# Seams between the stages of a four-layer network: the last weight slots by halves, turned rows of one half made meanwhile, mixers begun from rows without the root, layers unrolled

## The reference

```python
x = x + 0.5 * swiglu(rms_norm(x, g1), w_gate, w_up, w_down)      # FFN, 1024 -> 2816 -> 1024
x = x + mixer(rms_norm(x, g2))                                   # w_in, four branches or attention, w_out
x = x + 0.5 * swiglu(rms_norm(x, g3), ...)                       # a second FFN
```

## Time and profile before

| | |
|---|---|
| runs | 2213.47, 2214.14, 2214.24 us |
| median | 2214.14 us |
| profiled execution | 2215.12 us |
| its span, first to last instruction | 2213.3 us |
| TensorE matmuls busy | 2135.7 us, 96% |
| GpSimd busy | 1650.7 us, 75% |
| VectorE, ScalarE busy | 1015.2 us (46%), 996.0 us (45%) |
| HBM | 165 GB/s over the span |
| granted TensorE clock | 0.988 of full, mean |

### The profile page before, as it was taken

The page is one execution under the profiler, slowest core; times in us unless marked ns, Lnnn a source line. Parts: engine busy times, 40 slices in busy tenths (PEclk is TensorE's granted clock), DMA queues, the critical chain, the costliest instruction groups (busy, mean ns, idle before and its releaser), DMA issues.

```text
span 2213.3 us, 43461 instructions
## 1 busy us (share of the span) xinstructions
PE 2135.7 (96%) x15448; PEld 1965.4 (89%) x15448; DVE 1015.2 (46%) x1544; ACT 996.0 (45%) x1637; POOL 1650.7 (75%) x682
## 2 busy tenths in 40 slices
PE   7998999999999899999999989999999998999997
PEld 7998998999899898899899978889989997888997
DVE  3445545434443554434444454544444444454444
ACT  5344444434443544434444455444444445544343
POOL 6886855888788675688788854668878886466887
PEclk9999999999999999999999999999999999999999
DMA  6554533555455453455555543345555554334554
GB/s 223 189 180 154 183 116 123 189 182 188 155 187 182 153 172 115 143 182 188 180 171 186 169 163 111 130 153 187 182 179 164 188 174 162 108 132 153 189 181 142
DMA packets 101335, 365.72 MB, mean 165 GB/s; under 512 B 11888, under 2 KB 12528, under 8 KB 100976
## 3 DMA queue, kind: packets, MB, share of 16 engines
q1 hardware_dynamic: 101088, 363.20, 49.9%
q10 hardware_dynamic: 144, 1.19, 0.1%
HBM read 363.29 MB, written 1.05 MB: 165 GB/s over the span
## 4 chain that ended last, share of the span: by engine, by line
PE 92%; DVE 3%; issue 2%; ACT 2%; DMA 0%; SPq 0%; ACTq 0%; DVEq 0%
PE twin L559 19%; PE twin L561 18%; PE twin L560 18%; PE twin L593 9%; PE twin L594 9%; PE twin L595 8%; PE twin L680 1%; PE twin L574 1%; PE twin L663 1%; PE twin L575 1%; PE twin L576 1%; DVE stat L1459 1%; PE twin L606 1%; DVE stat L1461 1%; PE twin L669 1%
## 5 line engine op out<-in xcount | busy, mean ns | idle before, releaser
L524 POOL TENSOR_TENSOR wlo<-raw,whi 128x1024 fp32r<-128x1024 f32 x678 | 1650.5, 2459 | 554.3 <-ACT whi L1143 553.5
L559 PE MATMUL twin<-thi,whi 128*128 128x256 f32 x3504 | 1000.4, 286 | 14.7 <-DVE tlo L1475 14.7
L561 PE MATMUL twin<-thi,wlo 128*128 128x256 f32 x3504 | 992.0, 283 | 0.0
L560 PE MATMUL twin<-tlo,whi 128*128 128x256 f32 x3504 | 991.5, 283 | 0.0
L1143 ACT CAST whi<-raw 128x1024 fp32r<-128x1024 f32 x686 | 696.4, 1044 | 45.9 <-PE twin L595 28.7
L559 PEld LDWEIGHTS twin<-thi,whi 128*128 128x128 f32 x3504 | 672.6, 192 | 27.8 <-issue 19.5
L560 PEld LDWEIGHTS twin<-tlo,whi 128*128 128x128 f32 x3504 | 672.4, 192 | 8.8 <-issue 1.0
L561 PEld LDWEIGHTS twin<-thi,wlo 128*128 128x128 f32 x3504 | 672.2, 192 | 0.0
L1515 DVE TENSOR_TENSOR hlo<-mix,hhi 128x256 fp32r<-128x256 f32 x176 | 393.4, 2235 | 133.9 <-ACT hhi L1192 133.9
L1188 ACT ACTIVATE mix<-mix 128x256 f32<-128x256 f32 x176 | 73.6, 418 | 815.7 <-DVE mix L1510 815.7
L1510 DVE TENSOR_TENSOR mix<-twin,root 128x512 f32<-128x512 f32 x176 | 121.7, 692 | 618.9 <-PE twin L561 607.3
(11 more groups left out here) (265 smaller groups left out, 1468.3 us busy)
## 6 DMA issues: line engine op xcount, KB each, us to landing
raw<-in_w_dram SPq DMA_DIRECT2D x686, 512.0 KB, 3.3
con<-in_con_dram ACTq DMA_DIRECT2D x1, 1161.5 KB, 7.9
x<-in_x_dram SPq DMA_DIRECT2D x1, 1024.0 KB, 4.8
out_dram<-xs SPq DMA_DIRECT2D x4, 256.0 KB, 2.7
mix<-in_last_gain_dram SPq DMA_DIRECT2D x1, 512.0 KB, 3.5
par<-in_par_dram SPq DMA_DIRECT2D x2, 208.0 KB, 3.1
par<-in_par_dram SPq DMA_DIRECT2D x2, 154.0 KB, 3.0
gain<-in_gain_dram SPq DMA_DIRECT2D x5, 12.0 KB, 2.8
```

Of the source, the lines that this page charges most:

```text
L524: nc.gpsimd.tensor_tensor(wlo[:, place, :], raw[:, place, :], whi[:, place, :].bitcast(F32), ALU.subtract).then_inc(split_done, 1)
L559: pe.matmul(out, hi, thi[:, k, :], start=(k == 0), stop=False)
L560: pe.matmul(out, hi, tlo[:, k, :], start=False, stop=False)
L561: mm = pe.matmul(out, lo, thi[:, k, :], start=False, stop=(k == KD - 1))
```

## The change: what it does, and the diff

- **Tail.** The last three down slots of an FFN (19, 20, 21) are put behind gate/up 21, and run half 0 of all three, then half 1 of all three; the same for the last two slots of w_out. After the first of them has done its half 1, TensorE turns half 0 of the new x (8 transposes). Step 21 keeps its rows in a third place of `hhi`/`hlo`. In the very last FFN the slots run by token tile instead (`last_tail`).
- **Head.** The first two slots of each stage run in four parts: slot 0's lower four k, the 8 transposes of half 1, slot 1's lower four k, slot 0's and slot 1's upper four k. Turned rows of w = 1 and 2 go to `yhi`/`ylo` and new tiles `ehi`/`elo`.
- **Root.** The chain works in a PSUM bank but for its result, and has four small instructions more; squares come behind the upper parts of their half. The root is spread from `stat` itself, without a diagonal, in the middle of slot 2.
- **Mixers.** They begin like an FFN, from rows with gain but without the root, for slots 0 to 3; their results are multiplied by the root afterwards in PSUM (`rooted`). Meanwhile the turned x, still in its banks, is multiplied by gain and root and split again (`normalised`), and slots 4 on use that. Convolutions, rotations and pairs of the start come 2 to 4 slots later; in the second mixer the compressed k and v tile comes before the gates.
- **Ring and layers.** The ring's left-out places are spread over the mixer; GpSimd splits all slots; the four empty slots are gone. The loops over layers are written out; the loops inside the FFNs stay, one turn shorter.
- **End.** Per token tile: add, square, root, wait for the last gain, two results.

```diff
-TAIL = AHEAD
-IP_BANK1 = [5 + m % 2 for m in range(CHUNKS1 // 2)]
+IP_BANK1 = [6, 5, 4, 7] + [5 + m % 2 for m in range(4, CHUNKS1 // 2)]
-SHARED = [[FFN_SLOTS, FFN_SLOTS + 2], [FFN_SLOTS, FFN_SLOTS + 2]]
+SKIPS = {MIX1: (8, 14, 20, 26), MIX2: (8, 14, 22)}
...
+            def head(L, w, n, out):
+                ready = lambda j: early_ready(pe, L, w, j)
+                first, second = out[:, 0:SEQ], out[:, SEQ:2 * SEQ]
+                low, high = range(KD // 2), range(KD // 2, KD)
+                wait_slot(L, n)
+                fm_part(L, n, first, low, w, True, False, ready)
+                x_turned(L, w, 1)
+                wait_slot(L, n + 1)
+                fm_part(L, n + 1, second, low, w, False, False)
+                fm_part(L, n, first, high, w, False, True, ready).then_inc(slot_used, 1)
+                fm_part(L, n + 1, second, high, w, False, True).then_inc(slot_used, 1)
+            def root_spread(L, w, name):
+                out = claim(pe, L, name)
+                pe.wait_ge(ev("root_ready"), 3 * L.deep + w + 1)
+                for T in range(NT):
+                    mm = pe.matmul(out[:, T * P:(T + 1) * P], stat[:, T:T + 1].to_broadcast([P, P]), ident, start=(T == 0), stop=True,
+                                   skip_group_check=True)
+                full(L, name, mm)
...
+            def tail(L, slots, acc, next_norm):
+                last = slots[-1][0]
+                for half in range(2):
+                    for n, ahi, alo, inputs_ready in slots:
+                        if half == 0:
+                            inputs_ready()
+                            wait_slot(L, n)
                         for T in range(NT):
+                            mm = acc_part(L, n, ahi, alo, acc, half, T, False, n == last)
+                        if half == 1:
+                            mm.then_inc(slot_used, 1)
+                            if n == slots[0][0]:
+                                x_turned(*next_norm, 0)
...
+                head(L, 2 * f, base, bank[b])
+                gate_up(2, 1, 0, midway=lambda: root_spread(L, 2 * f, ("R", f)))
                 down(4, 0, first=True)
-                with pe.Fori(0, STEPS // 2 - 1) as i:
+                with pe.Fori(0, STEPS // 2 - 2) as i:
                     gate_up(5, 0, i + 1, i)
                     down(7, 1, i)
                     gate_up(8, 1, i + 1, i)
                     down(10, 2, i)
-                down(FFN_SLOTS - 1, STEPS - 1, last=True)
+                gate_up(FFN_SLOTS - 7, 0, STEPS // 2 - 1)
+                gate_up(FFN_SLOTS - 5, 1, STEPS // 2 - 1)
...
+            def norm(L, w, soon):
+                upper_x(L, w, 0)
+                for n in soon:
+                    split_hi(L, n)
+                squares(L, w, 0)
+                upper_x(L, w, 1)
+                squares(L, w, 1)
+                split_hi(L, ffn_slot(L, w))
+            def normalised(L):
+                root_kept(L, ("R", "mix"))
+                for j in range(KD // 2):
+                    act.wait_ge(ev("rescaled"), 4 * L.deep + j + 1)
+                    nc.scalar.copy(thi[:, 2 * j:2 * j + 2, :], psum(L, ("norm", 1, j))[:].rearrange("p (k n) -> p k n", k=2)).then_inc(ev("upper_again"), 1)
+                    if j < 3:
+                        split_hi(L, FFN_SLOTS + AHEAD + 1 + j)
...
-                step(0, STEPS - 2, STEPS // 2 - 1, (n - 2,), (n - 1, n) if f else (n - 1,))
-                step(1, STEPS - 1, STEPS // 2 - 1, (), (n + 1, n + 2, n + 3) if f else ())
+                step(0, STEPS - 2, STEPS // 2 - 1, (n - 2,), (n - 1,) if last else (n - 1, n))
+                step(1, STEPS - 1, STEPS // 2 - 1, (), () if last else (n + 1, n + 2), at=2 * SEQ)
...
+            def roots(own, squares_done, ready, scratch, tiles=range(NT)):
+                dve.wait_ge(sq_done, squares_done)
+                n, first = len(tiles), tiles[0]
+                zero, v, t, vh = (scratch[:, 2 * i:2 * i + n] for i in range(4))
+                y = stat[:, first:first + n]
...
+            def norm(L, own, w, added=None):
+                for half in range(2):
+                    if added is not None:
+                        add_to_x(*added, half)
+                    lower_x(L, w, half)
+                roots(own, L.deep * (6 * NT) + (w + 1) * 2 * NT, ev("root_ready"), bank[7])
+            def normalised(L):
+                wait_drained(dve, L, ("R", "mix"))
+                def scaled(j):
+                    out = psum(L, ("norm", 1, j))
+                    for c in range(2):
+                        part = out[:, c * SEQ:(c + 1) * SEQ]
+                        ins = dve.scalar_tensor_tensor(part, part, gain_of(L, 1, 2 * j + c), root[:], ALU.mult, ALU.mult)
+                    ins.then_inc(ev("rescaled"), 1)
+                def lower(j):
+                    dve.wait_ge(ev("upper_again"), 4 * L.deep + j + 1)
+                    drained(L, ("norm", 1, j), dve.tensor_tensor(tlo[:, 2 * j:2 * j + 2, :], psum(L, ("norm", 1, j))[:].rearrange("p (k n) -> p k n", k=2),
+                                                                 thi[:, 2 * j:2 * j + 2, :].bitcast(F32), ALU.subtract))
+                scaled(0)
+                for j in range(1, KD // 2):
+                    scaled(j)
+                    lower(j - 1)
+                lower(KD // 2 - 1)
+            def rooted(own, L, m):
+                out = psum(L, ("ip", m))[:].rearrange("p (t n) -> p t n", t=2)
+                own.link(dve.tensor_tensor(out, out, root[:].unsqueeze(1).to_broadcast([P, 2, SEQ]), ALU.mult))
...
             for T in range(NT):
                 for half in range(2):
+                    add_to_x(end, lambda T, half: ("acc", 1, T, half), 0.5, half, (T,))
+                roots(own, 2 * DEPTH * 6 * NT + 2 * (T + 1), ev("last_root"), bank[4], (T,))
+                dve.wait_ge(ev("last_root"), T + 1)
+                dve.wait_ge(s_par, 16 * 2 * DEPTH + 16)
+                for half in range(2):
                     cols = slice(half * 512, half * 512 + 512)
```

More of the change, by code:

```diff
@@ L444, in build @@
         y_moba = xs[:].rearrange("p t n -> p (t n)")[:, 1024:2048]
+        layers = [Layer(l, blk) for blk in range(2) for l in range(DEPTH)]
+        behind = dict(zip(range(len(layers)), layers[1:]))
         block = ctx.enter_context(nc.Block())
@@ L496, in _ @@
             sp.dma_start(gain[:], gain_d[0]).then_inc(s_gain, 16)
-            with sp.Fori(0, DEPTH) as l:
-                layer(l, 0)
-            with sp.Fori(0, DEPTH) as l:
-                layer(l, 1)
+            for blk in range(2):
+                for l in range(DEPTH):
+                    layer(l, blk)
             last = Layer(DEPTH, 1)
-            for n in range(TAIL):
-                load(last, n)
             sp.wait_ge(slot_used, last.slot0 + RING)
@@ new lines, in fm_part @@
+            def fm_part(L, n, out, ks, w, start, stop, ready=None):
+                r = L.pos[n] % RING
+                for k in ks:
+                    xhi, xlo = turned_x(w, k)
+                    if ready is not None and k % 2 == 0:
+                        ready(k // 2)
+                    hi, lo = whi[:, r, k * P:(k + 1) * P], wlo[:, r, k * P:(k + 1) * P]
+                    pe.matmul(out, hi, xhi, start=start and k == 0, stop=False, skip_group_check=True)
+                    pe.matmul(out, hi, xlo, start=False, stop=False, skip_group_check=True)
+                    mm = pe.matmul(out, lo, xhi, start=False, stop=stop and k == KD - 1, skip_group_check=True)
+                return mm
@@ new lines, in last_tail @@
+            def last_tail(L, slots, acc):
+                last = slots[-1][0]
+                for T in range(NT):
+                    for n, ahi, alo, inputs_ready in slots:
+                        if T == 0:
+                            inputs_ready()
+                            wait_slot(L, n)
+                        for half in range(2):
+                            mm = acc_part(L, n, ahi, alo, acc, half, T, False, n == last)
+                        if T == NT - 1:
+                            mm.then_inc(slot_used, 1)
@@ L1456, in roots, with lower_x @@
                 for step in range(3):
-                    for T in range(NT):
-                        c = slice(T, T + 1)
-                        own.step(dve.scalar_tensor_tensor(t[:, c], y[:, c], vh[:, c], y[:, c], ALU.mult, ALU.mult))
-                    own.wait()
-                    ins = dve.scalar_tensor_tensor(y, t, 1.5, y, ALU.add, ALU.mult)
-                    if step == 2 and ready is not None:
-                        ins.then_inc(ready, 1)
-                        dve.wait_ge(ready, own.L.each)
-                    else:
-                        own.link(ins)
-                return y
-            def remainders(L, w):
-                for j in range(KD // 2):
+                    own.link(dve.tensor_tensor(t, vh, y, ALU.mult))
+                    own.link(dve.tensor_tensor(t, t, y, ALU.mult))
+                    if step < 2:
```

(4 more changed lines are left out.)

449 lines of the change are left out of this document (216 added, 233 removed).

## The result

The kernel after takes **2176.01 us** (median of four runs, 2175.85 to 2176.86) against 2213.9 for the kernel before beside it (four runs, 2213.47 to 2214.24): ratio 0.983, 95% interval 0.9813 to 0.9847. The forecast was 2183.5, the range 2168 to 2199. The profiled execution spans 2174.0 us, so the span lost 39.3 us where the sum had 30.6.

What follows compares the result with a forecast made beforehand. TensorE busy 96% of the span, savings only at seams, start and end. Gains 21.4 (mixer heads) + 12.3 (FFN heads) - 3.1 (start and end) = 30.6 us off median 2214.14: 2183.5 us, range 2168 to 2199.

Steps and rivals of the forecast that it cites:

- (a): FFN tails by halves: TensorE waits 1.6 us for the last hlo at seven tails, 11 us; bounds 0.7 and 12.
- Rival A: Tail does not meet GpSimd, so the 11 us come too: 2173 us; chance 0.18.
- (b): Stage heads: upper four k about 0.3 us late behind an FFN; all waits 1.2 us behind a mixer.
- (c): Root at seams: PSUM chain takes 3.0 us, no wait; bound 24 us if a 2.3 us stall came back.
- (d): Rescaled rows in mixers: waits 1.8 us, gate logits' source 0.8 us late in first mixers; bound 0 to 3 us more.
- (e): GpSimd takes back the 8 slots VectorE split, 2.46 us each: costs nothing.
- (f): Layers unrolled: the layer loop's two turns cost 3.4 us together, counted inside the FFN seams' 22.8 us.
- (g): Start: 8 transposes now stand between matmuls at the low clock, 1.8 us; loss 0.5 us.
- (h): End: VectorE waits for the last gain before taking up tile 1; loss 2.6 us, bounds 0 and 4.
- Rival B: Start of the mixers costs 3 us more each: 2195 us, or 2200 with a late root; chance 0.21.
- Rival C: Mixers' 12 VectorE rescaling instructions stuck behind GpSimd's splits, 2.0 us more each, 96 us: 2279 us; chance 0.05.
- Rival D: Seams do not shorten, each wait goes to the next producer: within 4 us of 2214; chance 0.04.

Runs made afterwards that it cites:

- e1: Kernel after with the next stage's first weight split moved behind step 21, leaving two splits, not three, behind step 20: 2164.67 us, ratio 0.9778.
- e6: Kernel after with the 8 transposes of half 1 ahead of the first slot's matmuls, not between them: 2191.6 us, ratio 0.9894.
- e3: Kernel after with the root's chain in SBUF scratch again, not in a PSUM bank: 2199.19 us, ratio 0.9935.
- e4: Kernel before with only its loops over layers written out: 2206.26 us, ratio 0.9966.
- e10: Kernel after, unchanged, run once more in a second set: 2175.71 us, ratio 0.9831.
- e2: Kernel after with the last gain asked for 12 slots before the end, not behind the last slot: 2172.97 us, ratio 0.9816.
- e5: Kernel after with the last slots run whole, slot by slot, and half 0 turned only behind the last: 2185.06 us, ratio 0.987.
- e8: Kernel after with the edits of e1 and e2, and tile 1's adds between tile 0's root and its results: 2160.17 us, ratio 0.9758.
- e7: Kernel after with the head's rescaling taken out, so mixers wait for the root and all slots use rescaled rows: 2221.66 us, ratio 1.0036.

## Why the prediction was right, and where it was not

The sign, the mechanism and the range held, and the row that the forecast was built around came as told. The sum was short by 8.7 us (39.3 for 30.6), and that it was not short by more is luck: some 16 us came that it had not counted on, and some 7 went that it had not counted either. By its steps:

**(a) Tail by halves: right, to 0.1 us.** The step had to choose between a wait of 0.1 and one of 1.6 us, and took 1.6; the excess is 1.63 to 1.70 seven times, hlo took 2.06 us, and e1 shows that GpSimd was the cause. The choice between the two ends was made by where the batch stood in the earlier trace rows, and that is what decided. Rival A did not happen; that 2176.0 lies nearer to its 2173 than to 2183.5 is because of other terms.

**(b) Head: mis-sized, in the safe direction.** The 0.3 us behind an FFN is 0.15, at the first of the upper four k (213.40 and not 213.25, 0.05 us after `elo` is released), and the 1.2 us behind a mixer is 0.85 (0.27 at the first slot, 0.43 at the transposes, 0.15 at the upper four k): 7 x 0.15 + 4 x 0.35 = 2.4 us more gain. e6 shows that the head by quarters is needed for it.

**(c) Root: right.** The root is there 0.5 us before TensorE wants it, where the sum had 0.3. The "nothing" that this step cost was worth 23 us: e3 takes it back.

**(d) Rescaled rows: right in mechanism, too dear.** The four pairs were put 3.3, 4.8, 6.4 and 8.2 us behind the spread; they are ready after 3.4, 4.9, 6.3 and 7.7. The term that was too dear is the cycle of a pair, 0.44 + 0.44 + 0.69 = 1.57 us: the instructions overlap by 0.06 to 0.08 us each, and the `tlo` rows start 1.40 to 1.44 us apart. TensorE also comes to the first pair 4.7 us behind the spread (222.53) and not 4.3. Waits are 0.82 us in a first mixer (0.20 at 224.17, 0.62 at 225.60) and 0.97 in a second, and not 1.8, so 3.6 us in four mixers; the wait for the gate logits' source, 0.8 us in the two first mixers, isn't in the list: 1.6. The step also said that "the second mixer's rotations make their dates". There something was missed. L709 is the matmul that opens a bank of scores with the mask, L719 turns the exponentials that ScalarE makes of the scores (L1431). In the two second mixers they stand idle for 5.3 us in 10 pieces. The lines of before that answer to them are L653 and L663; the first had 1.5 us in 2 pieces (further down the list of the earlier trace rows), the second none. With 0.16 us a piece that is 6.9 against 1.8: 5.1 us against. This was a step passed without a number, and no run here takes it apart.

**(e) GpSimd's eight slots: right.** No row of the mixers waits for GpSimd; the only wait for wlo is at the start.

**(f) Unrolling: the sum held, its price was seen wrong.** It was put inside the 22.8 us and told as 3.4 us. e4 alone gives 7.2. The seams' sum was unhurt, because it was taken from all waits there and not from the "issue" row; the start's part was missed. The Trainium skill (Runtime: NRT & Kernel Launch, Instruction fetch mechanics) says that a taken branch to code outside the small window must fetch it before execution goes on; this fits the direction of e4, but no run here shows that the fetch is the cause. The amount at one turn, 3.1 us, is from the rows above.

**(g) Start: wrong in sign.** A loss of 0.5 us was forecast. The first gate matmul comes at 15.74 and not at 17.62, and 12 weight matmuls go at half clock and not 27, against which stand the transposes between (18.44 to 19.59). The 144th gate or up matmul starts at 38.90 and not 40.70: 1.8 us gained, so 2.3 us more than forecast. In e4 it starts at 39.18, in e10 at 39.19: 1.5 us goes with the unrolled code, and not with the order of squares that this step argued about. The shorter spell is not in e4, which again has 27 slow matmuls, and its cause was not found.

**(h) End: right, 1.0 us too dear.** From the last matmul's start to the end it was 12.9 us and is 14.4; forecast loss 2.6, measured 1.5 to 1.6. e2 shows that the late gain was its cause: 3.0 us come back.

**Two terms outside the steps.** One is a gain. In the kernel after, matmuls of 256 columns that read the new tiles `yhi`, `ylo`, `ehi` and `elo` (the first slots of a mixer, and every gate and up slot of the FFN behind it) follow one another after 118.3 to 118.4 ns on average, those that read `thi` and `tlo` after 119.6, as all of them did before (119.58 over 10172 of them). That is 1.2 ns for each of 4468, 5.4 us. It holds in the traces of e1, e5 and e8 too and not in e4, which has no such tiles; why the tile makes a difference is open.

The other was lost in the kernel before already. The sum took the first mixer's 12 slow matmuls for all four. Here are 2.2 us from just behind the first w_in matmul of each (engines' busy time and count, then the granted clock):

```profile
219.40:221.60 2.20, 2.20 (x13) 2.20 (x12) 2.20 (x6) 2.20 (x5) 0.31 (x1) 0.50 0.80 320
760.90:763.10 2.20, 2.20 (x21) 2.20 (x20) 2.20 (x6) 2.20 (x5) 0.30 (x1) 0.99 0.76 305
1298.50:1300.70 2.20, 2.20 (x14) 2.20 (x13) 2.20 (x6) 2.18 (x5) 0.30 (x1) 0.60 0.77 311
1853.30:1855.50 2.20, 2.20 (x21) 2.20 (x20) 2.20 (x6) 2.18 (x5) 0.31 (x1) 1.00 0.79 311
```

From the last matmul of the stage to the 25th w_in matmul the four seams lost 9.6, 8.6, 9.4 and 8.6 us, so 2.2 us of the 39.0 were not there to be gained.

**Together**, by steps (b), (d) twice, (g) and (h): 2.4 + 3.6 + 1.6 + 2.3 + 1.0 = 10.9 us not counted on, and 5.4 from the matmuls' pitch; 5.1 against in the second mixers and 2.2 in the seams of before. That makes 9.0 where the sum was short by 8.7. The closeness should not be taken for more than it is: pieces of 0.1 us, which TensorE loses at the matmul behind many a wait (213.62, 224.39), are counted on neither side.

**The signs.** Of those for right, the rows for hlo, the clock and the mixers' rows came; the fifth slot's wait is half of its 1.8 us, and the end comes 1.5 and not 2 to 3 us later. Of those for wrong, one came by the letter: there are new "issue" rows, L709 with 2.0 us and L665 with 1.1. They do not show that straight code costs. The four pieces of L665 stand behind the four mixers at the transposes that need VectorE's adds (e6 names that wait `DVE x L1568`), and the pieces of L709 at an instruction that waits for a semaphore, at the kind of place where e4 has "issue" and the kernel before has ScalarE.

**Rival B** fell with the margins in (c) and (d). **Rival C** did not happen, and its argument stands in one row: all rows of the form, VectorE's rescaling (count, then shortest, median and longest in ns), with GpSimd at work for 76% of the span.

```profile
L1587 DVE SCALAR_TENSOR_TENSOR twin<-twin,gain,root x32: 482/484/493, 219.0 to 1824.1; 128x256 f32<-128x256 f32 x32
```

```profile
L1593 DVE TENSOR_TENSOR tlo<-twin,thi x16: 682/691/693, 220.6 to 1825.9; 128x512 fp32r<-128x512 f32 x16
```

Beside them, the hlo rows, with both inputs in SBUF, have 425, 2434 and 2452 ns. **Rival D** is what e7 shows for the mixers alone: without the early start the waits go to the next producer one for one, and somewhat more.

**Where the 38 us come from**, as each part is missed when it alone is taken out: mixers without the root 45.7, chain in PSUM 23.2, head by quarters 15.6, tail by halves 9.0, unrolling 7.2 (put in alone). They do not add up to 38: a part that is taken out leaves a wait open that the others can no longer cover.

## What to carry to other kernels

When a seam is filled with matmuls, the price list changes from waits to dates: write for every producer when it is ready and when it is wanted, to a tenth of a microsecond, and look at what GpSimd is doing at that date. By e3, a small chain on VectorE that must be on time is better off in PSUM when GpSimd works beside it, and by e1 a batch of GpSimd splits should leave a gap where VectorE has one instruction on SBUF to make. And a wait that is accepted on the critical path (here the 1.6 us) is worth asking which single neighbour causes it: moving one weight split by one step gave 11.3 us, more than a quarter of the whole change again.

## What the runs showed of the hardware that was not expected

**The clock after short waits.** In e6 a wait of 2.36 us (excess over pitch) behind a mixer was followed at three of four places by 9 to 16 matmuls at 1.2 GHz, while 1.7 us at eleven seams of e5 and 1.65 us at seven tails of after left the clock at 1.00; and so did, in the kernel before, 1.61, 2.51 and 1.25 us one behind the other at a loop's turn (1.00 from 553 to 568). The same wait need not bring the same spell: in the kernel before, 6.8 us of idle and 16 transposes at half clock stand before each of the four mixers, and a further 11 slow matmuls, 1, 9 and 1. At the start, 7.7 us of idle before and 7.9 after were followed by 27 and by 12 slow weight matmuls. What sets the one and the other apart stays open.

**The turn of a hardware loop over layers** is felt on every engine that waits for another one: 3.1 us at a seam, of which the trace names 1.5 to 1.9 as "issue".

**The pitch of a matmul depended on the tile it read:** 118.3 to 118.4 ns from start to start with `yhi`, `ylo`, `ehi`, `elo` (four k each), 119.6 with `thi`, `tlo` (eight k each), both at a granted clock of 1.00.

**Size is no protection:** in e3 a VectorE instruction of 128x2 elements stood 2.41 us for a GpSimd split of 2.39, at twelve seams of twelve.
